# A two-layer diffusion step: 80 conditioning sums spread over four places instead of three, and one SiLU moved behind the first query copy

## The chip, the cores and the metric

The kernel runs on one core of a Trainium2 chip. The metric is the device time of one execution in microseconds (us); lower is better. The kernel has hand-written instruction streams for the engines: TensorE (PE in the profile), VectorE (DVE), ScalarE (ACT), GpSimd (POOL) and SyncE (SP). They meet only at semaphores. SP, ACT and POOL also issue DMAs.

## The reference, cut to what matters

A sequence of 128 prompt tokens and 256 latent tokens goes through two layers. Layer 0 has an mLSTM mixer, layer 1 a Mamba-2 (SSD) mixer, and each is followed by a mixture of experts. Every sub-layer is modulated by vectors that come from a conditioning vector:

```python
for i in range(DEPTH):
    mp = (jax.nn.silu(c_ctx) @ ada_w[i] + ada_b[i]).reshape(6, D_MODEL)   # prompt stream
    ms = (jax.nn.silu(c) @ ada_w[i] + ada_b[i]).reshape(-1, 6, 1, D_MODEL)  # latent stream
    hp = xp * (1.0 + mp[1]) + mp[0]
    ...   # mixer: mLSTM (i = 0) or SSD (i = 1)
    xp = _layer_norm(ALPHA * xp + mp[2] * yp, ln_w[i, 0], ln_b[i, 0])
    fp = _hier_moe(xp * (1.0 + mp[4]) + mp[3], *wm)
    xp = _layer_norm(ALPHA * xp + mp[5] * fp, ln_w[i, 1], ln_b[i, 1])

def _mlstm_mixer(h, ...):
    xu, z = jnp.split(h @ w_in, 2, axis=-1)
    xc = jax.nn.silu(_dwconv(xu, conv_w, conv_b))
    q, k, v = blockdiag(xc, w_q), blockdiag(xc, w_k), blockdiag(xu, w_v)
    gates = jnp.concatenate([q, k, v], axis=-1) @ w_gates + b_gates
    ...
```

The first mixer's shift and scale need two of layer 0's six vectors; those are made by TensorE at the start. The other ten vectors of 1024 numbers (four of layer 0, six of layer 1), for both streams, are the subject of the change.

## The kernel before, in words

**The conditioning sums.** The ten vectors are cut into 80 slabs of 128 outputs. A slab is a 128x1024 piece of the transposed weight (512 KB), and VectorE makes its 128 outputs for a stream as one multiply of the slab with the SiLU of the conditioning row, summed along the row by the same instruction (L1925). So a slab costs two such instructions, one per stream, each waited for. `summed(place, n)` does the next n slabs; `biased(l, j0, j1)` adds the bias to finished entries. POOL issues the loads: `columns(place)` (L1368) first loads the two conditioning rows (`c_rows`, 1 MB since they are spread to 128 partitions), then each slab into one of four slots of the place, and slab i may be issued only when sum i-3 is done. ScalarE makes the SiLU of the rows once for each place (`c_silu`, L1545).

There are three places, with `COLUMNS = (14, 42, 24)` slabs, each with its own rows and slots in parts of the arena that are free at that time:

- place 0: during the first mixer's up-projection and convolution, one slab behind each of the convolutions 1 to 14;
- place 1: four slabs ahead of, sixteen inside (one for each channel tile) and twenty-two behind the loop that multiplies the mLSTM's output with its gate, so during the z projection and the down-projection of the first mixer;
- place 2: during the down-projection of the second mixer.

In place 1 the slab whose index is a multiple of four goes to a slot that also holds the row of normaliser states; POOL waits for that row's DMA to the output (`out_mn`) before it issues such a slab.

**The first mixer's front.** TensorE projects 16 channel tiles of `xu` two at a time (L581). For each, ScalarE copies the tile out of PSUM and makes the middle tap (L1538 to L1543), VectorE adds four taps (L1949), ScalarE applies SiLU (L1534, L1535). When the projection is done, TensorE makes q, k and v of tile 0 and 1 and then, for each tile, gate products (L866), a transpose of v (L872) and q, k, v of the tile after next (L882, L886). The gate products of tile c wait for the copies of q and v by ScalarE (L1564, L1568) and of k by VectorE (L1961). ScalarE's stream is in order: the SiLU of tile 15 stands ahead of the first copy of q. POOL builds the block-diagonal weights (L1387).

**The first mixer's end.** TensorE projects z (L581), with two transposes of the mLSTM output behind each pair; VectorE combines them (L2113, L2117) and does a sum. Then the down-projection (L601) goes over two halves of 512 outputs and three token tiles; `gate_rows` (L625) stands three steps into it and needs VectorE's `diagonals` (L2138). VectorE's sums of the last 22 slabs stand ahead of `mixed(0)`, which takes the down-projection's banks, adds the residual and normalises (L2169 to L2153); TensorE then transposes the result (L633). PSUM banks are claimed in a ring of five or six; a claim waits for the last reader of what the bank held.

**The second mixer's front.** The residual comes from the experts; L1646 (ScalarE) and L2187 (VectorE) write the modulated input. TensorE projects 24 tiles of B, C and x in twelve steps (L581); behind the first stands the step-size projection (L1040), behind the fourth the transposes `columns()` (L1052 to L1058), which need VectorE's chain of softplus, scans and `rows_done` (L2445 to L2476). VectorE does a convolution per tile (L1949), ScalarE the copies and SiLU. ScalarE's wait for the softplus input (L1743) stands right behind `a_neg` (L1741). Meanwhile POOL multiplies and shifts the residual stream by the norm's weights (`new_x(1)`, L1398 and L1399, six instructions) and clears the convolution's pads.

SP issues the weight slabs into a ring of six (L1300) and the experts' weights (L1239, L1266). It waits for the sums of the first two places before it loads experts' slab 5 of layer 0.

## Time and profile before

| | |
|---|---|
| median of 3 runs | 1394.72 us (1389.98 to 1398.69) |
| profiled execution, its own time | 1389.08 us |
| its span, first to last instruction | 1387.2 us |
| mean granted TensorE clock | 0.932 of full |
| PE busy | 1214.7 us (88%) |
| DVE busy | 707.3 us (51%) |
| ACT busy | 369.0 us (27%) |
| POOL busy | 207.2 us (15%) |
| DMA | 290.17 MB, mean 209 GB/s |

All row times are microseconds from the span's start. A timeline row is: start, length, engine, line, operation, output<-input, count, and in brackets the idle time of the engine ahead of it with what ended it. A chain row is: start, length, what the end of the execution was waiting for at that time. The busy share is an average over stages; what counts below is which wait ends last in each stage.

### The profile page before, as it was taken

To read this page: it belongs to the slowest core of one execution; us is meant where nothing else is said; L and a number is where in the kernel's file an instruction comes from. 1 tells how busy PE (TensorE), PEld (TensorE's weight loads), DVE (VectorE), ACT (ScalarE), POOL (GpSimd) and SP (SyncE) were. 2 spreads that over 40 slices of the span, in tenths; PEclk is the share of its full clock that TensorE was granted. 3 is DMA by queue.
4 is the path that set the end of the run, shared out by engine and by line. 5 is a ranking of instruction groups with operands and counts; after the bars stand their busy time and mean duration, and the time that the engine had idled before them with its cause. 6 is when DMAs were issued, how large, how long until landed. Compare 5 with 4: busy or idle time off the path is not lost.

```text
span 1387.2 us, 14709 instructions
## 1 busy us (share of the span) xinstructions
PE 1214.7 (88%) x5174; PEld 659.8 (48%) x5174; DVE 707.3 (51%) x1538; ACT 369.0 (27%) x808; POOL 207.2 (15%) x307
## 2 busy tenths in 40 slices
PE   5898978999999797899585999989998999899573
PEld 2554545554566343734222555656666444743221
DVE  0399244342476599541104365448885777541014
ACT  1433331222300000311013354444555211311011
POOL 5012200000010010002201401003334110002201
PEclk9999997999999899799798999999999899799796
DMA  9553001327397486299936332234435697399934
GB/s 375 191 192 135 1 1 49 114 108 260 128 388 256 153 345 245 89 415 422 420 155 219 137 122 84 93 107 152 141 126 170 214 381 297 129 416 421 421 146 149
DMA packets 75844, 290.17 MB, mean 209 GB/s; under 512 B 7692, under 2 KB 18188, under 8 KB 61436
## 3 DMA queue, kind: packets, MB, share of 16 engines
q1 hardware_dynamic: 41952, 191.12, 35.7%
q0 software_dynamic: 16352, 60.44, 11.8%
q10 hardware_dynamic: 17468, 37.67, 7.4%
q8 instruction: 42, 0.69, 0.2%
q14 instruction: 30, 0.25, 0.1%
HBM read 261.30 MB, written 27.90 MB: 208 GB/s over the span
## 4 chain that ended last, share of the span: by engine, by line
PE 63%; DVE 12%; DMA 11%; issue 9%; ACT 4%; SPq 1%; POOL 0%; ACTq 0%; POOLq 0%; DVEq 0%
PE bank L581 19%; PE bank L740 7%; PE bank L601 7%; DMA arena<-in_moe_gu 4%; PE bank L949 4%; DVE arena L1925 3%; PE bank L760 3%; PE bank L1136 3%; DMA ring<-in_ada_w 3%; DVE arena L2501 2%; DVE arena L1949 2%; PE bank L840 2%; PE bank L882 1%; DMA ring<-in_b_w_out 1%; PE bank L977 1%
## 5 line engine op out<-in xcount | busy, mean ns | idle before, releaser
L581 PE MATMUL bank<-hT,ring 128*128 128x384 f32 x896 | 297.9, 494 | 3.8 <-ACT hT L1525 1.7
L581 PEld LDWEIGHTS bank<-hT,ring 128*128 128x128 f32 x896 | 172.0, 194 | 122.0 <-issue 6.8
L601 PE MATMUL bank<-ring,arena 128*128 128x512 f32 (+1 forms) x512 | 178.2, 614 | 9.1 <-DVE arena L2113 7.3
L1925 DVE SCALAR_TENSOR_TENSOR arena<-arena 128x1024 f32<-128x1024 f32 x112 | 137.3, 1226 | 6.9 <-DMA arena<-in_ada_wT 4.2
L740 PE MATMUL bank<-arena,hT 128*64 128x512 f32 x416 | 107.4, 637 | 34.0 <-DMA arena<-in_moe_gu 22.7
L1949 DVE SCALAR_TENSOR_TENSOR arena<-arena,par 128x388 f32<-128x388 f32 x160 | 101.6, 638 | 67.4 <-ACT arena L1543 62.8
L601 PEld LDWEIGHTS bank<-ring,arena 128*128 128x128 f32 (+1 forms) x512 | 73.9, 198 | 103.7 <-issue 87.0
L1136 PE MATMUL bank<-hT,ring 128*128 128x384 f32 x256 | 97.6, 507 | 0.8 <-ACT arena L1543 0.8
L740 PEld LDWEIGHTS bank<-arena,hT 128*64 128x64 f32 x416 | 37.7, 146 | 92.1 <-issue 86.5
L1380 POOL DMA_DIRECT2D arena<-in_ada_wT x74 | 39.1, 529 | 272.3 <-DVE arena L1925 266.1
L1470 POOL TENSOR_TENSOR arena<-arena 128x192 f32<-128x192 f32 x64 | 42.7, 697 | 214.0 <-PE bank L1169 156.7
L2317 DVE TENSOR_TENSOR arena<-arena,bank 128x256 f32<-128x256 f32 x16 | 6.7, 422 | 127.3 <-ACT arena L1669 127.3
L2569 DVE TENSOR_TENSOR arena<-arena 128x1024 f32<-128x1024 f32 x32 | 42.0, 1311 | 35.6 <-ACT arena L1814 35.6
L949 PE MATMUL bank<-ring,arena 128*128 128x512 f32 x128 | 58.3, 616 | 0.0
L1136 PEld LDWEIGHTS bank<-hT,ring 128*128 128x128 f32 x256 | 44.8, 192 | 26.4 <-issue 8.7
L2501 DVE TENSOR_SCALAR arena<-arena 128x128 f32<-128x128 f32 x192 | 49.9, 328 | 4.0 <-PE bank L1169 4.0
L760 PE MATMUL bank<-arena 128*64 128x512 f32 x208 | 50.7, 592 | 0.0
L1925 DVE SCALAR_TENSOR_TENSOR arena<-arena,hT 128x1024 f32<-128x1024 f32 x36 | 44.1, 1224 | 3.4 <-DMA arena<-in_ada_wT 2.3
L1669 ACT ACTIVATE arena<-bank 128x256 f32<-128x256 f32 x16 | 6.1, 383 | 145.0 <-PE bank L740 145.0
L1810 ACT ACTIVATE arena<-arena 128x768 f32<-128x768 f32 x32 | 27.0, 844 | 66.1 <-DVE arena L2501 66.1
L840 PE MATMUL bank<-arena,hT 128*128 128x512 f32 x48 | 25.3, 692 | 19.6 <-DMA arena<-yg,slots 19.6
L949 PEld LDWEIGHTS bank<-ring,arena 128*128 128x128 f32 x128 | 25.0, 198 | 30.2 <-issue 30.1
(425 smaller groups left out, 1656.5 us busy)
## 6 DMA issues: line engine op xcount, KB each, us to landing
arena<-in_moe_gu SPq DMA_DIRECT2D x56, 1024.0 KB, 15.8
arena<-in_ada_wT POOLq DMA_DIRECT2D x74, 512.0 KB, 5.6
arena<-in_moe_dn SPq DMA_DIRECT2D x28, 1024.0 KB, 20.8
ring<-in_b_w_in SPq DMA_DIRECT2D x40, 512.0 KB, 3.5
ring<-in_a_w_in SPq DMA_DIRECT2D x32, 512.0 KB, 6.4
ring<-in_moe_gu SPq DMA_DIRECT2D x12, 1024.0 KB, 14.4
arena<-acs_rows ACTq DMA_DIRECT2D x32, 384.0 KB, 3.5
yg<-arena ACTq DMA_DIRECT2D x18, 512.0 KB, 8.1
```

What stands on the lines that cost most here:

```text
L581: last = mm(keys[j][1][:, 0:T], w[:, k, P * j:P * j + P], hT[:, 4 * half + k, :], start=half == 0 and k == 0, stop=half == 1 and k == 3, s ...
L601: last = mm(keys[t][1][p:p + tokens.shape[1], :], tokens, w[:, j, :], start=k == 0, stop=k == KE - 1, skip_group_check=True)
L740: last = mm(ps[CAP * u:CAP * u + CAP, :], m_hg[:, q % 2, P * k + CAP * u:P * k + CAP * u + CAP], v3(w[u][1], 4)[:, j, :], start=k == 0, st ...
L760: last = mm(ps[CAP * u:CAP * u + CAP, :], m_aT[:, P * f + CAP * u:P * f + CAP * u + CAP], v3(w[u][1], 2)[:, f, 512 * h:512 * h + 512], sta ...
L840: last = mm(ps[:, :], w_diag[:, t, i, :], m_y[:, i, t, 512 * half:512 * half + 512], start=i == 0, stop=i == 1)
L949: last = mm(keys[t - 1][1][:, :], a_qT[:, KH * h + 2 * half + j, P * t:P * t + P], w[:, j, :], start=half == 0 and j == 0, stop=half == 1 ...
L1136: last = mm(ps[:, 0:T], v3(w, 4)[:, k % 4, P * (c % 2):P * (c % 2) + P], hT[:, k, :], start=k == 0, stop=k == KD - 1, skip_group_check=True)
L1470: ins = pl.tensor_tensor(out=b_xdt[c % 2][:, d, :, PH * h:PH * h + PH], in0=b_x[:, :, P * c + PH * h:P * c + PH * h + PH], in1=b_col[:, o: ...
L1925: ins = ve.scalar_tensor_tensor(out=products, in0=c_slots[place][i % 4], scalar=1.0, in1=rows[:, v, :], op0=ALU.mult, op1=ALU.mult, accum_ ...
L1949: last = ve.scalar_tensor_tensor(out=dst, in0=src[:, j:j + W_PAD - 2 * PAD], scalar=w(j), in1=dst, op0=ALU.mult, op1=ALU.add)
L2501: ins = ve.tensor_scalar(b_E[:, h, d, P * t:P * t + P], b_row[:, m % 3, h, P * t:P * t + P], b_col[:, at:at + 1], 0.0, ALU.add, ALU.min)
L2569: ve.tensor_tensor(out=e, in0=e, in1=b_cb[:, g % 2, d, :].unsqueeze(1).to_broadcast([P, 2, 512]), op=ALU.mult).then_inc(sem("w_ready"), 1)
```

## The change

The 80 sums are done in four places, `COLUMNS = (12, 36, 8, 24)`. The order of the slabs stays.

- Place 0 has 12 slabs: convolutions 13 and 14 have none behind them.
- Place 1 has 36: four ahead of the gate loop, twelve inside it (every fourth tile has none), twenty behind it. Its first slab now has index 12, a multiple of four.
- A new place 2 has 8 slabs, in the second mixer's front: four right behind `modulated(1)` and ahead of the softplus chain, and one behind each of the convolutions 6 to 9. Their bias is added behind convolution 10. ScalarE's SiLU of the rows stands between `a_neg` and the softplus. POOL loads the rows and the first four slabs when the experts' results are gathered, ahead of `new_x(1)`; it loads the other four behind `new_x(1)` and the pads, and waits for all eight sums before it goes on to `xdt`.
- The former place 2 is place 3, with its 24 slabs as before.
- ScalarE's SiLU of tile 15 stands behind the first copies of q and v instead of ahead of them.

```diff
--- before.py
+++ after.py
@@ -200,13 +200,16 @@
         free = lambda o, n=D: arena[:, o:o + n]
         q_at = KE * T + KE * W_PAD
         gone_at, far_at = KE * T + 4 * D, ARENA - 7 * D
-        c_rows = [v3(a, 2) for a in (free(q_at, 2 * D), free(far_at + 5 * D, 2 * D), hT_free[:, 0:2 * D])]
-        c_products = (free(q_at + 2 * D), free(far_at + 4 * D), free(KE * T + 2 * D))
+        later = KE * T + 2 * G * T + NT * E2
+        e_at = later + NT * E2 + 2 * E2 + ZT * T + 3 * 2 * T + 2 * NT * P + T + 9 * 64
+        c_rows = [v3(a, 2) for a in (free(q_at, 2 * D), free(far_at + 5 * D, 2 * D), free(e_at, 2 * D), hT_free[:, 0:2 * D])]
+        c_products = (free(q_at + 2 * D), free(far_at + 4 * D), free(e_at + 3 * D), free(KE * T + 2 * D))
         c_slots = [[free(o + D * i) for i in range(4)] for o in (q_at + 3 * D, far_at)]
+        c_slots.append([free(o) for o in (later - D, later + 2 * P * KD, e_at - T - 9 * 64 - 2 * NT * P - 2 * T, e_at + 2 * D)])
         c_slots.append([free(gone_at), free(gone_at + D), hT_free[:, 2 * D:3 * D], free(ARENA - 12 * MSLAB)])
-        COLUMNS = (14, 42, 24)
+        COLUMNS = (12, 36, 8, 24)
         column_of = [(place, l, j) for place, (l, j) in zip(
-            [p for p in range(3) for _ in range(COLUMNS[p])], [divmod(2 * KD + i, 48) for i in range(80)])]
+            [p for p in range(4) for _ in range(COLUMNS[p])], [divmod(2 * KD + i, 48) for i in range(80)])]
         COLUMN_SEMS = ("pool_in0", "pool_in1", "pool_in2", "xc_in0")
 
         def column_landed(i):
@@ -216,7 +219,7 @@
 
         def columns_in(l, j):
 
-            return 16 * len(range(j, sum(COLUMNS[0:2 + l]), 4))
+            return 16 * len(range(j, sum(COLUMNS[0:2 + 2 * l]), 4))
 
         def rows_landed(l, t):
 
@@ -1365,13 +1368,14 @@
 
             pool.wait_ge(sem("small_in"), SMALL)
 
-            def columns(place):
+            def columns(place, n0=0, n1=None):
 
                 first = sum(COLUMNS[0:place])
-                pool.wait_ge(sem("small_in"), SMALL + 16 * place)
-                pool.dma_start(c_rows[place].rearrange("p v k -> p (v k)"),
-                               i_["c_rows"].to_broadcast([P, 2 * D])).then_inc(sem("small_in"), 16)
-                for i in range(first, first + COLUMNS[place]):
+                if n0 == 0:
+                    pool.wait_ge(sem("small_in"), SMALL + 16 * place)
+                    pool.dma_start(c_rows[place].rearrange("p v k -> p (v k)"),
+                                   i_["c_rows"].to_broadcast([P, 2 * D])).then_inc(sem("small_in"), 16)
+                for i in range(first + n0, first + (n1 or COLUMNS[place])):
                     _, l, j = column_of[i]
                     if i >= 4:
                         pool.wait_ge(sem("summed"), i - 3)
@@ -1456,9 +1460,14 @@
                 pool.wait_ge(sem(f"out{s}"), 16 * OUT_C)
             columns(1)
             moe(0)
+            for t in range(NT):
+                pool.wait_ge(*rows_landed(0, t))
+            columns(2, 0, 4)
             new_x(1, range(NT))
             pl.memset(b_cbuf.rearrange("p k t -> p (k t)"), 0.0)
             pl.memset(b_pre.rearrange("p k t -> p (k t)"), 0.0).then_inc(sem("pads"), 1)
+            columns(2, 4)
+            pool.wait_ge(sem("summed"), sum(COLUMNS[0:3]))
 
             def xdt(c):
                 pool.wait_ge(read("xt"), c + 1)
@@ -1489,7 +1498,7 @@
             pool.wait_ge(sem("xdt_ready"), 2 * KE)
             pool.wait_ge(sem("wx_ready"), 2 * G)
             pool.wait_ge(filled, group["in", 3 * KE - 1][1])
-            columns(2)
+            columns(3)
             moe(1)
 
 
@@ -1557,7 +1566,6 @@
                     conv_silu(c - 1, a_cbuf[:, (c - 1) % 2, :], a_cb(c - 1), a_xc[:, c - 1, :], "xc_ready")
                 if c == 0:
                     c_silu(0)
-            conv_silu(KE - 1, a_cbuf[:, (KE - 1) % 2, :], a_cb(KE - 1), a_xc[:, KE - 1, :], "xc_ready")
 
             for c in range(KE):
                 ps = await_bank(act, "qT", c)
@@ -1566,6 +1574,8 @@
                 if c >= 2:
                     act.wait_ge(filled, group["v", c - 2][1])
                 ac(a_vb[:, c % 2, :], ps[:, 0:T], ACT.Copy).then_inc(read("vT"), 1)
+                if c == 0:
+                    conv_silu(KE - 1, a_cbuf[:, (KE - 1) % 2, :], a_cb(KE - 1), a_xc[:, KE - 1, :], "xc_ready")
 
 
             act.wait_ge(sem("softplus_x"), 1)
@@ -1739,6 +1749,7 @@
             modulated(1, 2)
 
             ac(a_neg[:, :], a_log[:, :], ACT.Exp).then_inc(sem("dt_a"), 1)
+            c_silu(2)
             act.wait_ge(sem("softplus_x"), 2)
             link(ac(b_u, b_u, ACT.Exp))
             ac(b_l, b_u, ACT.Ln, bias=1.0).then_inc(sem("softplus_ln"), 1)
@@ -1859,9 +1870,9 @@
                 if m >= 26:
                     new_state(m - 26)
             z_silu(12, 15)
-            c_silu(2)
             new_state(6)
             new_state(7)
+            c_silu(3)
             for c in range(10, KE):
                 normed(c)
             scaled(KE - 1)
@@ -1953,9 +1964,9 @@
             for c in range(KE):
                 dve.wait_ge(read("in"), c + 1)
                 conv(c, a_xu[:, c, :], a_cbuf[:, c % 2, :], lambda j: a_cw(j, c), "conv_ready")
-                if 0 < c < KE - 1:
+                if 0 < c < 13:
                     summed(0, 1)
-            biased(0, 16, 30)
+            biased(0, 16, 28)
             for c in range(KE):
                 ps = await_bank(dve, "kT", c)
                 ve.tensor_copy(a_kT[:, c, :], ps[:, 0:T]).then_inc(read("kT"), 1)
@@ -2115,7 +2126,8 @@
                 dve.wait_ge(read("hn"), c + 1)
                 dve.wait_ge(read("in"), KE + c + 1)
                 ve.tensor_tensor(out=xc, in0=xc, in1=a_sz[:, c, :], op=ALU.mult).then_inc(sem("gA_ready"), 1)
-                summed(1, 1)
+                if c % 4 != 3:
+                    summed(1, 1)
 
             def columns(n):
 
@@ -2433,12 +2445,13 @@
             dve.wait_ge(sem("out_mn"), 32)
             dve.wait_ge(sem("x_in"), 16 * (MAXOQ + 1))
             diagonals(0)
-            summed(1, 22)
-            biased(0, 30, 48)
-            biased(1, 0, 24)
+            summed(1, 20)
+            biased(0, 28, 48)
+            biased(1, 0, 16)
             mixed(0, "yA")
             moe(0)
             modulated(1)
+            summed(2, 4)
 
 
             ps = await_bank(dve, "single", 3)
@@ -2548,6 +2561,10 @@
                 w = 16 + c if c < 8 else c - 8
                 dve.wait_ge(read("xbc"), c + 1)
                 conv(c, b_pre[:, c % 4, :], b_cbuf[:, c % 3, :], lambda j: b_cw(j, w), "conv_ready")
+                if 6 <= c < 10:
+                    summed(2, 1)
+                if c == 10:
+                    biased(1, 16, 24)
                 if c == 4:
                     rows_done()
                 elif c == 5:
@@ -2587,12 +2604,12 @@
             dve.wait_ge(sem("c_in"), 16 * (1 + OUT_S))
             dve.wait_ge(sem("par_in"), 16 * (2 + OUT_S))
             diagonals(2, (0, 1))
-            summed(2, 12)
+            summed(3, 12)
             diagonals(2, (2, 3))
-            summed(2, 2)
+            summed(3, 2)
             ps = await_bank(dve, "single", 4)
             ve.tensor_scalar(rms, ps[:, 0:NT], float(D) / E2, EPS, ALU.mult, ALU.add).then_inc(read("single"), 1)
-            summed(2, 10)
+            summed(3, 10)
             biased(1, 24, 48)
             dve.wait_ge(sem("sqrt_ready"), 2)
             link(ve.reciprocal(rms, rms))
```

## Rows read from the trace of the kernel before

**Rows 1.** The page: shares of the span in the chain that ended last.

```profile
PE 63%; DVE 12%; DMA 11%; issue 9%; ACT 4%; SPq 1%; POOL 0%; ACTq 0%; POOLq 0%; DVEq 0%
```

**Rows 2.** Chain of waits, end of the first mixer's convolutions.

```profile
137.79 0.40 ACT arena L1534
...
138.59 0.37 ACT arena L1564
138.96 0.39 ACT arena L1568
```

**Rows 3.** Timeline there, VectorE and ScalarE.

```profile
124.67 2.60 DVE L1949 SCALAR_TENSOR_TENSOR arena<-arena,par 128x388 f32<-128x388 f32 x4
127.19 1.22 DVE L1925 SCALAR_TENSOR_TENSOR arena<-arena 128x1024 f32<-128x1024 f32 x1
...
127.45 0.49 ACT L1543 ACTIVATE arena<-bank,par 128x256 f32<-128x256 f32 x1
...
130.03 0.49 ACT L1543 ACTIVATE arena<-bank,par 128x256 f32<-128x256 f32 x1
```

**Rows 4.** Timeline of TensorE, the gate products that follow.

```profile
139.59 1.50 PE L866 MATMUL bank<-arena,gates_w 128*32 128x384 f32 x6 [6.15 <-ACT arena L1568]
...
145.05 0.85 PE L866 MATMUL bank<-arena,gates_w 128*32 128x384 f32 x6
...
148.26 0.85 PE L866 MATMUL bank<-arena,gates_w 128*32 128x384 f32 x6
```

**Rows 5.** Windows there: PE, PEld, DVE, ACT, POOL busy (x), clock, DMA, GB/s.

```profile
139.60:141.70 2.10, 2.10 (x9) 0.86 (x10) 0.00 (x0) 0.50 (x2) 0.00 (x0) 0.50 0.00 0
```

**Rows 6.** Timeline, start of place 1: POOL, VectorE, TensorE.

```profile
372.80 1.06 POOL L1380 DMA_DIRECT2D arena<-in_ada_wT  x2
380.06 1.05 POOL L1380 DMA_DIRECT2D arena<-in_ada_wT  x2 [6.20 <-DMA out_n<-arena]
...
387.41 1.23 DVE L1925 SCALAR_TENSOR_TENSOR arena<-arena 128x1024 f32<-128x1024 f32 x1 [2.99 <-DMA arena<-in_ada_wT]
...
400.32 10.49 PE L581 MATMUL bank<-hT,ring 128*128 128x384 f32 x32
```

**Rows 7.** Timeline, the first down-projection: VectorE and TensorE.

```profile
482.51 0.69 DVE L2138 TENSOR_TENSOR arena<-ident,mod 128x512 f32<-128x512 f32 x1 [11.43 <-PE bank L625]
...
485.07 60.25 PE L601 MATMUL bank<-ring,arena 128*128 128x512 f32 x140
552.35 1.97 PE L633 MATMUL bank<-ident,x_tok 128*128 128x128 f32 x8 [7.03 <-DVE x_tok L2153]
554.11 5.20 PE L601 MATMUL bank<-ring,arena 128*128 128x512 f32 x8
```

**Rows 8.** Timeline, second mixer's front: VectorE's gap, ScalarE, POOL.

```profile
783.02 0.61 DVE L2445 TENSOR_SCALAR arena<-bank,dt_bias 64x384 f32<-64x384 f32 x1 [16.80 <-PE bank L1040]
...
767.53 0.20 ACT L1741 ACTIVATE a_neg<-a_log 64x1 f32<-64x1 f32 x1
...
776.75 2.35 POOL L1399 TENSOR_TENSOR x_tok<-x_tok,arena 128x1024 f32<-128x1024 f32 x1
```

**Rows 9.** Timeline and chain: VectorE and POOL on the arena together.

```profile
113.26 2.18 POOL L1387 TENSOR_TENSOR arena<-arena 128x128 f32<-128x128 f32 x6
...
113.11 2.76 DVE arena L1949
...
131.57 5.10 POOL L1387 TENSOR_TENSOR arena<-arena 128x128 f32<-128x128 f32 x6 [16.13 <-PE bank L886]
...
132.32 1.41 DVE L1925 SCALAR_TENSOR_TENSOR arena<-arena 128x1024 f32<-128x1024 f32 x1
```

**Rows 10.** Timeline, what TensorE's fifth projection step needs.

```profile
810.34 0.28 DVE L2476 TENSOR_TENSOR arena<-arena 64x128 f32<-64x128 f32 x1
...
812.28 0.49 ACT L1543 ACTIVATE arena<-bank,par 128x256 f32<-128x256 f32 x1
...
814.77 20.91 PE L581 MATMUL bank<-hT,ring 128*128 128x384 f32 x64
```

## The prediction

> **What bounds the kernel now.** I read the chain of waits first. Two thirds of the span hang on TensorE and only 12% on VectorE [rows 1], so the 80 slab sums matter only in the stages where VectorE is the last to arrive. There the timelines of all engines show who waits. Two such places are emptied by the change, and a third is filled.
>
> One slab costs 2.53 us of VectorE: a sum starts at 127.19, and the convolution behind it can start at 129.71 [rows 3].
>
> **Front of the first mixer (a gain).** The chain runs through VectorE's last convolution, then ScalarE's SiLU of tile 15 from 137.79 and its first copies of q and v, to 139.35 [rows 2]; TensorE then starts its gate products at 139.59, after 6.15 us of idling [rows 4]. Without the sums behind convolutions 13 and 14 the taps are held back by their input instead. ScalarE frees tile 14 at 127.45 + 0.4 = 127.9 and tile 15 at 130.03 + 0.4 = 130.4 [rows 3]. Convolution 15 then takes 2.5 us (124.67 to 127.19, [rows 3]) and ends at 133.0, against 137.8 before. Behind the new order ScalarE copies q and v of tile 0 while VectorE still works on tile 15, at about 131.3 to 132.2, so the last to arrive is VectorE's copy of k: bias 0.2, copy 0.55 (lengths from the timeline), 133.8. The gate products start at 133.85 instead of 139.59: 5.7 us. Of these 4.7 are the two sums and about 1 is the moved SiLU, which stood as 0.8 us ahead of 0.75 us of copies [rows 2].
>
> There is a second part. Behind the 6.15 us of idling TensorE ran at a granted clock of 0.50, the level of 1.2 GHz [rows 5], and its first round took 145.05 - 139.59 = 5.46 us against 3.21 for the next, at full clock [rows 4]. TensorE would be busy until 133.4 and idle for 0.4 us only, so I expect no fall: 2.2 us more (0 if it falls anyhow). Together **-7.9 us** (bounds -5.7 and -7.9; the loop behind it is a TensorE loop of 3.2 us per tile and passes the gain on).
>
> **Start of place 1 (a loss).** Before, POOL issued slabs 14 and 15 at 372.80 and had to wait for the state row's DMA only for slab 16, at 380.06 [rows 6]. Now the first slab is number 12, a multiple of four, so nothing but the rows is issued before 380.06, and 13, 14, 15 stand in POOL's queue behind that wait. Slab 16 landed at 387.4, 7.3 us after its issue: VectorE waited 2.99 us for it [rows 6]. Slab 12 will land then, and VectorE, which before had two sums behind it by 387.4, has all four ahead of it: it enters the gate loop at 397.7 instead of 392.5. In the loop VectorE has 3.7 us of idling in each pair and tile 3 now has no sum (2.5 us), so it catches up by tile 4. But the projection step at 400.4 [rows 6] needs the bank that VectorE frees in tile 1, at 397.7 + 3.7 + 0.6 = 402.0 (0.6 is the combining instruction). TensorE waits for it: **+1.6 us**. Below, 0: if the lone slab lands 2 us sooner. Above, 4: if the following slabs, with DMA engines full, land late once more each. The nearest row is the 7.3 us, hence 1.6.
>
> At the loop's end nothing is won: tiles 12, 13, 14 have the same sums as before, and TensorE waits for tile 14's bank. The sum saved behind tile 15 only lengthens VectorE's idle 11.43 us ahead of the diagonals [rows 7].
>
> **Behind the first down-projection (a gain).** From 484 to 541 VectorE does 22 sums in one row, while TensorE's projection ends at 485.07 + 60.25 = 545.3 [rows 7]. `mixed(0)` follows, 10.8 us to the first normalised tile, and TensorE idles 7.03 us until 552.35 [rows 7]. Twenty sums end 2 x 2.53 = 5.1 us sooner. The first token tile's second half is projected by 538.4, before VectorE comes to it (543.7), so the whole 5.1 us arrive, and 2.0 us of idling stay. SP's wait for the first two places' sums comes 5.1 us sooner too. The clock again: the eight records behind the idling took 5.20 us [rows 7] where eight at the projection's pace of 60.25 / 140 = 0.43 take 3.4. VectorE's next tile is ready only 5.1 us sooner, so of this at most 1.4 can be used; I take half: **-5.8 us** (-5.1 to -6.5).
>
> **Second mixer's front (the price).** VectorE has 16.80 us of nothing there, until TensorE has the step sizes at 783.02 [rows 8]. Four sums are 10.1 us. Their slabs and rows, 3 MB, are issued from 750.3 on, when the gathered results have landed and DMA engines are empty; they are there by 762. ScalarE's SiLU costs a table load (1.28) and 1.91 us (as in place 1) behind 767.53 + 0.20 [rows 8]: VectorE starts at 771.0, and without anything else it would end at 781.1. These 10.1 us would be free.
>
> But POOL works through `new_x(1)` until 779.1 [rows 8], 2.35 us per instruction, on SBUF operands like VectorE's. When six of POOL's small instructions ran back to back for 2.18 us, a tap of 0.63 took 2.76: VectorE lost all of POOL's time [rows 9]. When VectorE was in sums, POOL was the one that waited (5.10 for the same six), and a sum lost 0.19 [rows 9]. Here POOL has 8.0 us left at 771, and VectorE's eight instructions outlast it. Bounds for VectorE's loss are 4 x 0.19 = 0.8 and 8.0 us. I take 7.5: POOL's instructions are long, two stand back to back, and each lets one of VectorE's through at most.
>
> The Trainium skill, SBUF - State Buffer, section "SBUF: two separate sides", says that a VectorE instruction with two SBUF inputs and a GpSimd one that reads SBUF exclude each other for a whole instruction, whoever was first, and that the loser is blocked fully. By it the loss would be the full 8.0 us; the sum that lost only 0.19 beside a POOL instruction of 0.36 shows less than that.
>
> VectorE ends at 788.6 and the softplus chain is 5.5 us late. It is a chain through ScalarE and back, and up to convolution 5 it has almost no idling, so all of it moves. TensorE has slack: `rows_done` was ready at 810.6 for a use at 814.1 (3.5 us), and tile 6, whose bank the fifth step needs, was copied at 812.28 + 0.49 = 812.8, for a start at 814.8 (2.0 us) [rows 10]. So TensorE waits 5.5 - 2.0 = 3.5 us: **+3.4 us** (bounds 0 and 4.5).
>
> The other four sums, behind convolutions 6 to 9, add 10.1 us. VectorE idles 3.24, 5.14 and 5.56 us ahead of convolutions 8, 10 and 12 (timeline), 13.9 in all. Worked through tile by tile, with 5.5 us of lateness TensorE's 3.5 us of waiting make room, and convolution 12 starts when its input comes. Their cover is this idling; without it they would cost what VectorE overruns. Their slabs are issued at about 784 and needed from 818. POOL's wait for all eight sums ends at about 840, and its first `xdt` needs a transpose of that time anyway. Bias 0.2 us: hidden. The other place-3 work is as before. Zero.
>
> **The sum** against the profiled execution's own 1389.08: -7.9 + 1.6 - 5.8 + 3.4 = -8.7, so 1380.4. That execution stood 5.6 us below the median shown; against the median of 1394.72 it is **1386 us**, -0.6%. What a measurement of this kernel can tell from no change is about 1%, 14 us; the three runs alone spread over 8.7.
>
> **Rivals.**
> - *POOL and VectorE don't hold each other up* (the sum that lost 0.19 speaks for it, the tap that lost 2.13 against). The second mixer's front costs nothing, and with the start of place 1 at 0 to 1.6 the whole is -12.1 to -13.7: 1381 to 1382.6. Chance 0.25.
> - *Given back*: the sums in place 1 start late and stay late (slabs 16 to 19 took 7.3 to 10.6 us to land), TensorE waits in two or three of its steps instead of one (+4), the clock falls as before (the 2.2 and the 0.7 are lost), and the front costs its 4.5. Then -5.7 + 4 - 5.1 + 4.5 = -2.3: 1392. Chance 0.16.
> - *Slower*: the second mixer's front becomes bound by VectorE. Place: convolutions 6 to 12. Price: all eight sums, 20.3, and POOL's 8.0 on TensorE's path, less the 13.4 won elsewhere: about +15, 1410. It decides if VectorE reaches convolution 12 later than its input, which from the sums above needs over 5 us more than I count. For it: VectorE and ScalarE pass each other every tile there. Against it: 13.9 us of idling in the same stretch. Chance 0.07.
> - My forecast (1382 to 1390) has the remaining 0.52.
>
> **Numbers.** The range takes the rivals of gain, the bounds, and 4 us of scatter of the median: 1376 to 1397; only the slow rival lies outside. Faster by over 1% (below 1380.8): half of the first rival, and a tenth of the forecast for scatter and unused clock gains, and the tails: 0.23. Slower by over 1%: 0.07. Within: 0.70.
>
> **What would show it.** (1) The idling ahead of the first gate products shrinks from 6.15 to under 1 us, and the first round takes 3.2 us. (2) The first sum of place 1 starts at the new time that answers to 387.4, and one z step waits for VectorE. (3) Idling ahead of the first L633 is about 2 us. (4) In the second mixer's front VectorE's sums beside `new_x(1)` have instructions of 3 us and more, and the softplus input comes about 5.5 us behind TensorE's step sizes; TensorE waits once ahead of its fifth step. The prediction is wrong if those sums run at 1.22 us each, if a stage behind them (the experts) takes back what was won, or if TensorE waits for VectorE in convolutions 8 to 12.

## The result and the profile after

The changed kernel takes 1374.55 us (median of 4 runs, 1373.22 to 1377.01) against 1394.43 for the kernel before in the same comparison: ratio 0.986, interval 0.983 to 0.989. Three later comparisons, on three chips, gave 0.987 (0.985 to 0.990), 0.989 (0.986 to 0.992) and 0.989 (0.987 to 0.992). On the four chips of the experiments the kernel before has a median of 1391.5 us (74 runs; 1391.7 with the four of the first comparison), and the kernel after, over all its 21 runs, one of 1375.0. So the change is worth 16.6 us, 1.2%. I had predicted 1386, 8.7 us less than before, and the result lies 1.5 us below my range.

The page of the profiled execution (span 1375.2, own time 1377.01), first the chain that ended last; line numbers are 3 to 13 higher than before.

```profile
PE 60%; DMA 12%; DVE 12%; issue 9%; ACT 5%; SPq 1%; POOL 0%; ACTq 0%; POOLq 0%; DVEq 0%
```

Nothing has moved by much against [rows 1]: TensorE is still the bound. The change shows in single waits. **The first gate products**, timeline of TensorE, start, length, line and, in brackets, the idle time before:

```profile
134.40 0.85 PE L869 MATMUL bank<-arena,gates_w 128*32 128x384 f32 x6 [0.74 <-issue]
...
137.60 0.85 PE L869 MATMUL bank<-arena,gates_w 128*32 128x384 f32 x6
```

They answer to [rows 4]: 0.74 us of idling in place of 6.15, and the first round takes 3.20 us where it took 5.46. Its six matmuls last 0.85 us instead of 1.50, the length that they have at the full clock. **The start of place 1**, POOL, VectorE and TensorE:

```profile
372.18 2.28 POOL L1384 DMA_DIRECT2D arena<-in_ada_wT  x4 [6.04 <-DMA out_n<-arena]
...
380.08 1.22 DVE L1936 SCALAR_TENSOR_TENSOR arena<-arena 128x1024 f32<-128x1024 f32 x1 [7.29 <-DMA arena<-in_ada_wT]
...
395.83 1.56 PE L584 MATMUL bank<-hT,ring 128*128 128x384 f32 x4 [1.48 <-DVE arena L2124]
```

Against [rows 6] POOL issues all four slabs in one go behind its wait, VectorE waits 7.29 us for the first, and one z step waits 1.48 us for a bank. **The first down-projection**, TensorE, answering to [rows 7]:

```profile
543.61 1.31 PE L636 MATMUL bank<-ident,x_tok 128*128 128x128 f32 x8 [3.58 <-DVE x_tok L2165]
544.72 5.13 PE L604 MATMUL bank<-ring,arena 128*128 128x512 f32 x8
```

The same place in the trace of after_again, a second profiled execution of the changed kernel (experiment 1):

```profile
540.77 1.12 PE L636 MATMUL bank<-ident,x_tok 128*128 128x128 f32 x8 [1.74 <-DVE x_tok L2165]
541.73 3.60 PE L604 MATMUL bank<-ring,arena 128*128 128x512 f32 x8
```

3.58 or 1.74 us of idling are left of 7.03. The eight matmuls behind it took 5.20 us before; they take 3.60 where the granted clock is full (1.00 over that stretch of after_again), and 5.13 where it isn't (0.72 in the first trace). **The second mixer's front**, VectorE's eight sum instructions with POOL's `new_x(1)` beside them, the step sizes (L2458), and TensorE's wait ahead of its fifth step, answering to [rows 8, 10]:

```profile
761.43 2.04 DVE L1936 SCALAR_TENSOR_TENSOR arena<-arena 128x1024 f32<-128x1024 f32 x1 [4.79 <-ACT arena L1557]
763.51 3.24 DVE L1936 SCALAR_TENSOR_TENSOR arena<-arena 128x1024 f32<-128x1024 f32 x1
766.80 3.24 DVE L1936 SCALAR_TENSOR_TENSOR arena<-arena 128x1024 f32<-128x1024 f32 x1
770.09 3.25 DVE L1936 SCALAR_TENSOR_TENSOR arena<-arena 128x1024 f32<-128x1024 f32 x1
773.38 1.23 DVE L1936 SCALAR_TENSOR_TENSOR arena<-arena 128x1024 f32<-128x1024 f32 x1
...
778.45 0.61 DVE L2458 TENSOR_SCALAR arena<-bank,dt_bias 64x384 f32<-64x384 f32 x1
```

```profile
760.03 2.36 POOL L1402 TENSOR_TENSOR x_tok<-x_tok,arena 128x1024 f32<-128x1024 f32 x1
762.47 3.21 POOL L1403 TENSOR_TENSOR x_tok<-x_tok,arena 128x1024 f32<-128x1024 f32 x1
765.63 3.33 POOL L1402 TENSOR_TENSOR x_tok<-x_tok,arena 128x1024 f32<-128x1024 f32 x1
769.04 3.21 POOL L1403 TENSOR_TENSOR x_tok<-x_tok,arena 128x1024 f32<-128x1024 f32 x1
...
806.12 0.28 PE L1055 MATMUL bank<-ident,arena 64*128 64x64 f32 x1 [1.03 <-DVE arena L2489]
...
807.86 1.53 PE L584 MATMUL bank<-hT,ring 128*128 128x384 f32 x4 [0.97 <-ACT arena L1552]
```

Four of the eight instructions ran beside POOL and took 11.8 us instead of 4.9. TensorE then waits twice, 1.03 us for `rows_done` and 0.97 for its bank.

**Landmarks.** Each row is a stretch between two instructions of TensorE, in the us of one profiled execution of each kernel. "Before" has two executions and "after" four, so the last columns give the scatter too; "others" are experiments (below) that don't touch the stretch, or that have it as the kernel before has it where that is said.

| stretch, by the times of before | before | after | others |
|---|---|---|---|
| start to 194.3 (front) | 194.3, 195.6 | 186.8, 186.3, 186.2, 187.3 | old front 193.7, 194.9 |
| 194.3 to 366.4 (scan) | 172.1, 174.1 | 173.4, 172.9, 172.5, 174.1 | 172.0 to 173.9 |
| 366.4 to 400.3 (place 1 starts) | 33.9, 35.4 | 35.6, 35.7, 35.3, 35.6 | old order 33.8, 33.8 |
| 400.3 to 552.4 (to the router) | 152.0, 150.7 | 147.8, 145.9, 147.0, 146.0 | 22 sums 151.8 |
| 552.4 to 765.3 (experts 0) | 213.0, 214.9 | 212.1, 212.9, 213.5, 213.4 | 210.9 to 213.5 |
| 765.3 to 814.8 (step sizes) | 49.5, 49.9 | 52.1, 51.7, 52.1, 52.1 | no sums 49.4, 49.4 |
| 814.8 to 909.9 (convolutions) | 95.1, 95.1 | 95.1, 96.8, 95.1, 95.1 | 95.1, 96.8 |
| 909.9 to 1121.6 (end of mixer 2) | 211.7, 209.1 | 207.5, 207.7, 207.7, 207.9 | below |
| 1121.6 to the end (experts 1) | 265.6, 265.5 | 264.8, 263.3, 260.8, 266.4 | 263.5 to 268.5 |

The two profiled executions that were there first differ by 12.1 us only (1389.08 and 1377.01). The one of before lies 2.4 us below the median of its kernel, the one of after 2.0 above: this is the rest of the 16.6.

### The profile page after: what moved, and what is told of

It reads as the page before. It is cut to its first block, busy times and chain, and to the rows that moved or that the text cites. A ratio compares the mean times of both kernels' runs of the same rounds, so it can differ in the third digit from the quotient of the medians.

```text
span 1375.2 us, 14716 instructions
## 1 busy us (share of the span) xinstructions
PE 1206.2 (88%) x5174; PEld 654.0 (48%) x5174; DVE 712.4 (52%) x1539; ACT 373.3 (27%) x811; POOL 212.4 (15%) x308
## 3 DMA queue, kind: packets, MB, share of 16 engines
q0 software_dynamic: 16496, 61.49, 11.8%
## 4 chain that ended last, share of the span: by engine, by line
PE 60%; DMA 12%; DVE 12%; issue 9%; ACT 5%; SPq 1%; POOL 0%; ACTq 0%; POOLq 0%; DVEq 0%
PE bank L584 16%; PE bank L604 9%; PE bank L743 7%; DMA arena<-in_moe_gu 4%; PE bank L952 4%; PE bank L763 3%; PE bank L1139 3%; DMA ring<-in_ada_w 3%; DVE arena L1936 2%; DVE arena L2514 2%; PE bank L843 2%; PE bank L885 2%; DMA out_C<-arena 1%; PE bank L980 1%; DMA ring<-in_b_w_out 1%
## 5 line engine op out<-in xcount | busy, mean ns | idle before, releaser
L604 PE MATMUL bank<-ring,arena 128*128 128x512 f32 (+1 forms) x512 | 175.3, 608 | 8.9 <-DVE arena L2124 7.2
L1936 DVE SCALAR_TENSOR_TENSOR arena<-arena 128x1024 f32<-128x1024 f32 x112 | 144.1, 1287 | 19.0 <-DMA arena<-in_ada_wT 11.4
L1479 POOL TENSOR_TENSOR arena<-arena 128x192 f32<-128x192 f32 x64 | 42.8, 699 | 208.9 <-PE bank L1172 154.0
L2586 DVE TENSOR_TENSOR arena<-arena 128x1024 f32<-128x1024 f32 x32 | 41.7, 1304 | 35.3 <-ACT arena L1825 35.3
```

What stands on the lines that cost most here:

```text
L604: last = mm(keys[t][1][p:p + tokens.shape[1], :], tokens, w[:, j, :], start=k == 0, stop=k == KE - 1, skip_group_check=True)
L1479: ins = pl.tensor_tensor(out=b_xdt[c % 2][:, d, :, PH * h:PH * h + PH], in0=b_x[:, :, P * c + PH * h:P * c + PH * h + PH], in1=b_col[:, o: ...
L1936: ins = ve.scalar_tensor_tensor(out=products, in0=c_slots[place][i % 4], scalar=1.0, in1=rows[:, v, :], op0=ALU.mult, op1=ALU.mult, accum_ ...
L2586: ve.tensor_tensor(out=e, in0=e, in1=b_cb[:, g % 2, d, :].unsqueeze(1).to_broadcast([P, 2, 512]), op=ALU.mult).then_inc(sem("w_ready"), 1)
```

## The experiments

Sixteen runs, in four groups that each shared a chip and the runs of the kernel before. A ratio is to that kernel.

**1. Both kernels again.** No edit.

> The kernel before once more, unchanged, to learn how far its own executions differ. The profiled difference of the two kernels was 12.1 us, the difference of the medians 19.9. If the 7.8 us between them are scatter of the kernel before, its five rounds here lie between about 1389 and 1399 again, and its landmarks in the trace move in the stages that wait for DMA alone. If they are a real gain of the change that the two profiled executions happened not to show, the profiled execution here is at about 1395 and the landmarks of the first mixer are later than in the first trace.

> The kernel after once more, unchanged. Theory of the scatter: 1373 to 1379, a ratio of 0.987 to 0.991 (12 to 18 us). Rival, a real gain of 20: ratio 0.985 to 0.986.

Measured: 1391.59 (1.000, 0.998 to 1.002) and 1374.58 (0.987, 0.985 to 0.990), 17 us apart; their profiled executions, 1392.03 and 1374.96, are 17.1 apart. The landmarks of before are up to 3.3 us later at the end of the scan, and 1.5 more at the start of place 1. The gain is about 17 us, inside the 12 to 18 of the scatter theory; the interval doesn't rule out the rival's 0.986. So the 12.1 of the first pair of traces was chance, and so were the 19.9 of the first medians. Repeats of after, as partners on the chips of groups 3 and 4:

> The kernel after, unchanged, on the same chip as the three others: 1373 to 1378, ratio 0.986 to 0.989.

> The kernel after, unchanged, on the same chip as the others: 1372 to 1378.

Measured: 1375.39 (0.989, 0.986 to 0.992) and 1376.23 (0.989, 0.987 to 0.992).

**2. The last SiLU of the second mixer.** The diff moves it from ahead of `new_state(6)` and `new_state(7)` to behind them. Edit of silu_move_only, in the kernel before; silu_move_undone (and its repeat silu_undone_again) does the reverse in the kernel after.

```diff
             z_silu(12, 15)
-            c_silu(2)
             new_state(6)
             new_state(7)
+            c_silu(2)
```

> The kernel before with one edit: at the end of the second mixer its last SiLU over the gates stands behind the last two states on ScalarE instead of ahead of them. My theory of the miss: in the trace before, this SiLU waits 2.59 us for its data from DMA, the scaling of the last states queues behind it, and PE waits 3.07 for that; with the SiLU moved, the down-projection's first part starts about 6.7 earlier, 2.5 of it is given back at the gate's rows, whose diagonals then wait for DMA, and about 4.2 us stay: ratio 0.997, 2 to 6 us faster than before. Rival (the 4 us come from the sums that no longer run there, not from the SiLU): 0, within 1.5 us of before, and the first part of the down-projection starts where it did.

> The kernel after with this one edit undone: the last SiLU over the gates stands ahead of the last two states again. My theory: 4.2 us slower than after (2 to 6), ratio to before 0.991 to 0.994, and the scaling of the last states waits on ScalarE behind the SiLU. Rival (the SiLU's move is worth nothing without the sums' lateness): within 1.5 us of after.

> The kernel after with the second mixer's last SiLU ahead of its last two states again, repeated: the first time its median was 7.1 us above that of the kernel after on the same chip, while the two traces showed 3 to 5. If the SiLU's place is worth what the traces show (the states' products wait 3.8 us for ScalarE; some of it given back at the gate's rows), 3 to 5 us slower than after_third; rival, 7 again, because the idling also makes the clock fall in some executions that the profiled one does not show: then the mean granted clock of its timed runs is lower, by 0.003 or more, than that of after_third.

Measured: silu_move_only 1387.59 (0.997, 0.995 to 0.999) on the chip where before had 1391.89, so 4.3 us faster. silu_move_undone 1381.70 (0.993, 0.990 to 0.995) where after had 1374.58; the repeat 1379.87 (0.990, 0.989 to 0.992) where after had 1375.39, so 7.1 and 4.5 slower. Over the twelve runs its median is 1380.3, 5.4 above after's. In the trace of before_again, timeline of ScalarE and then of TensorE:

```profile
1079.13 1.91 ACT L1548 ACTIVATE hT<-hT 128x2048 f32<-128x2048 f32 x1 [2.49 <-DMA hT<-in_c_rows]
1080.94 0.58 ACT L1799 ACTIVATE arena<-bank 128x512 f32<-128x512 f32 x1
```

```profile
1081.67 1.36 PE L1119 MATMUL bank<-arena 128*128 128x128 f32 x8 [3.79 <-ACT arena L1799]
1082.82 1.91 PE L601 MATMUL bank<-ring,arena 128*128 128x512 f32 x2
```

The SiLU waits 2.49 us for its rows from DMA and runs 1.91. The state's copy (L1799) stands behind it in ScalarE's queue, TensorE waits 3.79 us for that copy, and the down-projection (L601) stands behind both. Nothing needs the SiLU at that point: VectorE reads it for sums that come later. The same stretch of silu_move_only:

```profile
1074.61 0.58 ACT L1799 ACTIVATE arena<-bank 128x512 f32<-128x512 f32 x1
...
1079.72 1.91 ACT L1548 ACTIVATE hT<-hT 128x2048 f32<-128x2048 f32 x1 [0.46 <-ACT arena L1799]
```

```profile
1076.71 1.92 PE L1119 MATMUL bank<-arena 128*128 128x128 f32 x8
1078.47 1.88 PE L601 MATMUL bank<-ring,arena 128*128 128x512 f32 x4
```

Here the wait is gone. The wait had a second cost: behind it the down-projection's first twenty matmuls ran at a lower granted clock. They are shown for the kernel before (0.75), then for the kernel after (1.00):

```profile
1079.44 7.26 PE L601 MATMUL bank<-ring,arena 128*128 128x512 f32 x20
```

```profile
1065.79 5.53 PE L604 MATMUL bank<-ring,arena 128*128 128x512 f32 x20
```

All five traces with the SiLU ahead show 7.01 to 7.27 us for them, twelve of the thirteen with it behind 5.53 and one 5.71. But not all of this arrives. Counted from 909.9 the down-projection begins at 162.9 us in the kernel after, at 166.8 and 167.0 with only the SiLU put back (silu_move_undone and its repeat), at 167.2 and 169.6 in the kernel before and at 166.4 in silu_move_only. So at that point the SiLU's place is worth some 4 us in the kernel after, and 2.8 are given back behind the down-projection's first part:

```profile
1107.20 3.43 PE L628 MATMUL bank<-arena,ones 128*128 128x512 f32 x4 [2.82 <-DVE arena L2150]
```

```profile
1074.84 1.29 DVE L2150 TENSOR_TENSOR arena<-ident,mod 128x512 f32<-128x512 f32 x2 [7.44 <-DMA out_s<-arena]
```

VectorE's diagonals (L2150) wait 7.44 us for the store of the last states, the gates' rows (L628) wait 2.82 for the diagonals, and this is the new bound of the place. From 909.9 to 1121.6 the five traces with the SiLU ahead show 208.8 to 211.7 us (mean 210.0), thirteen with it behind 207.5 to 209.6 (mean 207.9): 2.1 us. That mean mixes two kernels. In the kernel after alone the stretch takes 208.8 and 208.9 us with the SiLU ahead and 207.5 to 207.9 behind, 1.2 us. Counted from 909.9 to the end of the span the means of the five and the thirteen are 476.7 and 473.1, 3.6 us, but single traces overlap there (474.5 to 480.1 and 468.4 to 476.6). The timed effect is larger, 4.3 to 7.1. My second rival for that, a lower clock in runs that no trace shows, expected 0.003 between the means; the repeat had 0.941 against 0.942, the first run 0.940 against 0.942. So it is shown that the SiLU's place costs time and by which wait; the size is 1 to 4 us by the traces and 4 to 7 by the times, and where the difference lies stays open.

**3. The front of the first mixer.** front_undone is the kernel after with the old front, front_only the kernel before with the new one.

```diff
 front_undone, against after:
-        COLUMNS = (12, 36, 8, 24)
+        COLUMNS = (14, 34, 8, 24)
-                if 0 < c < 13:
+                if 0 < c < KE - 1:
-            summed(1, 20)
+            summed(1, 18)
...
 front_only, against before:
-        COLUMNS = (14, 42, 24)
+        COLUMNS = (12, 44, 24)
-                if 0 < c < KE - 1:
+                if 0 < c < 13:
-            summed(1, 22)
+            summed(1, 24)
```

In both the bounds of `biased` follow the sums, and the SiLU of tile 15 stands as in the front that they take over.

> The kernel after with the front of the first mixer as before: 14 sums behind its convolutions, the SiLU of tile 15 ahead of the first copies of q and v, and 18 sums instead of 20 behind the first down-projection (place 1 gets 34 slabs, its first is number 14). My theory of the front: TensorE idles 6 us again ahead of its first gate product, its clock falls for the first round, and the gates end 7.5 to 8 us later than in the kernel after. Behind the down-projection two sums fewer should take away the 1.7 to 3.6 us of idling that the kernel after still has there (the last to arrive is then TensorE), and place 1 starts as before, with two slabs issued ahead of the wait for the state row: -1.5. So 3 to 6 us slower than after: ratio to before 0.990 to 0.992. Rival (the front's gain is given back later, and the whole gain of the change lies in the second mixer and the down-projection): within 1.5 us of after, or faster.

> The kernel before with the front of the first mixer alone changed as in the kernel after: 12 sums behind its convolutions, the SiLU of tile 15 behind the first copies of q and v; the two slabs go to place 1 (44), as two more sums behind the first down-projection (24). My theory: the front gives 8 us (gates end at about 186.5 instead of 194.2 to 195.6), the start of place 1 takes 1.5 back, and VectorE's 24 sums in one row end two sums later than in the kernel before, so that 5 us go there: the idling ahead of the router's first transposes grows from 6.6 to about 12. In all 1 to 2 us faster than before: ratio 0.999. Rival, the down-projection's length is set by DMA and not by the sums: 6 to 7 us faster, 0.995.

Measured: front_undone 1380.03 (0.993, 0.991 to 0.995), front_only 1389.81 (0.9995, 0.998 to 1.001). The first lies just above the 0.990 to 0.992 of my theory, which its interval holds; it shuts out the rival. The second is near the theory's 0.999, and shuts out the rival's 0.995. TensorE's first gate products in the trace of front_undone:

```profile
139.11 1.50 PE L869 MATMUL bank<-arena,gates_w 128*32 128x384 f32 x6 [6.16 <-ACT arena L1577]
140.54 0.90 PE L875 MATMUL bank<-ident,arena 128*128 128x128 f32 x3
141.24 2.67 PE L885 MATMUL bank<-arena 128*128 128x384 f32 x4
```

Idling and the slow round are back together, and the first landmark comes at 193.7 against 186.2 to 187.3. In front_only it comes at 185.7, some 9 us earlier than in the kernel before. But ahead of the router's first transposes, TensorE in front_only:

```profile
554.01 1.97 PE L633 MATMUL bank<-ident,x_tok 128*128 128x128 f32 x8 [13.82 <-DVE x_tok L2154]
```

13.82 us of idling against 7.03 [rows 7]: that stretch takes 159.2 us instead of 151.5. The front's gain is a real one, and two slabs that are only pushed into the next place cost nearly all of it there: 7.7 us, and 1.4 at the start of place 1, of the 9. That eight slabs go on to a place of their own lets it arrive.

**4. The moved SiLU of tile 15.** Edit of qv_undone, in the kernel after:

```diff
+            conv_silu(KE - 1, ..., "xc_ready")
             for c in range(KE):
                 ps = await_bank(act, "qT", c)
...
-                if c == 0:
-                    conv_silu(KE - 1, ..., "xc_ready")
```

> The kernel after with one edit: the SiLU of tile 15 stands ahead of the first copies of q and v again. By the sum of the prediction this is worth about 1 us (VectorE's copy of k for the first tile is then not the last; 0.8 us of SiLU stands ahead of 0.75 us of copies): the first gate product 0.8 to 1 us later, and no fall of the clock. Rival: with 1.7 us of idling in place of 0.74 the clock falls for the first round as it did before, and 3 us are lost.

Measured: 1377.57 (0.990, 0.988 to 0.993). TensorE:

```profile
134.39 0.85 PE L869 MATMUL bank<-arena,gates_w 128*32 128x384 f32 x6 [1.58 <-ACT arena L1577]
```

1.58 us of idling against 0.74: 0.84 us, and the matmuls keep their 0.85. The rival is out.

**5. The start of place 1.** Edit of rotated, in the kernel after:

```diff
-        c_slots = [[free(o + D * i) for i in range(4)] for o in (q_at + 3 * D, far_at)]
+        c_slots = [[free(q_at + 3 * D + D * i) for i in range(4)], [free(far_at + D * ((i + 1) % 4)) for i in range(4)]]
-                    if place == 1 and i % 4 == 0:
+                    if place == 1 and i % 4 == 3:
```

> The kernel after with the slots of place 1 rotated by one, so that the slab that must wait for the state row's DMA is the fourth issued and no longer the first. Theory: the first sum of place 1 starts as VectorE comes free (7 us of waiting for its slab go), VectorE enters the gate loop earlier, and the z step that waits 1.5 us for its bank in the kernel after waits for nothing: -1.5 us, ratio 0.986. Rival: the later slabs land late instead, with the DMA engines as full as before, and nothing changes (within 0.5 us at the end of the z steps).

Measured: 1376.21 (0.991, 0.988 to 0.994), which tells nothing of 1.5 us. The trace does: POOL issues three slabs before the wait,

```profile
363.58 1.76 POOL L1384 DMA_DIRECT2D arena<-in_ada_wT  x3
372.25 0.53 POOL L1384 DMA_DIRECT2D arena<-in_ada_wT  x1 [6.91 <-DMA out_n<-arena]
```

VectorE starts its sums at 370.15 without waiting, no z step waits for a bank, and the stretch takes 34.0 us against 35.3 to 35.7 (with waits of 1.10 to 1.75) in the kernel after. A second trace with the rotation gave 33.9, a third 35.2 (both and packed, below), again with no wait. The third has its 1.3 us elsewhere: the first 64 matmuls of the stretch took 23.68 us instead of 22.40 and 22.57.

**6. POOL beside the sums.** Edit of no_new_x, in the kernel after:

```diff
-                    x = x_tok[:, t, :]
-                    link(pl.tensor_tensor(out=x, in0=x, in1=rows[:, 0, :], op=ALU.mult))
-                    pl.tensor_tensor(out=x, in0=x, in1=rows[:, 1, :], op=ALU.add)...
+                    x = x_tok[:, t, 0:8 if n == 1 else D]
+                    link(pl.tensor_tensor(out=x, in0=x, in1=rows[:, 0, 0:8 if n == 1 else D], op=ALU.mult))
+                    pl.tensor_tensor(out=x, in0=x, in1=rows[:, 1, 0:8 if n == 1 else D], op=ALU.add)...
```

> The kernel after, but POOL's new_x(1) works on 8 of 1024 columns: it leaves out nearly all of the scaling and shifting of the second mixer's residual rows. This takes POOL's work away from beside VectorE's sums and leaves everything else. Theory of the mutual hold-up: the sums' instructions are 1.23 us again instead of 3.24, VectorE ends 6.9 us earlier, the step sizes are no longer late, and TensorE's fifth step comes 2.7 us earlier: ratio 0.985. Rival (the instructions are longer for another reason, such as the slabs' landing in SBUF): they stay above 2 us and nothing moves.

Measured: 1376.03 (0.990, 0.988 to 0.992). VectorE's sums in its trace:

```profile
759.10 1.23 DVE L1936 SCALAR_TENSOR_TENSOR arena<-arena 128x1024 f32<-128x1024 f32 x1 [5.08 <-ACT arena L1557]
...
767.97 1.23 DVE L1936 SCALAR_TENSOR_TENSOR arena<-arena 128x1024 f32<-128x1024 f32 x1
...
771.67 0.61 DVE L2458 TENSOR_SCALAR arena<-bank,dt_bias 64x384 f32<-64x384 f32 x1 [2.47 <-PE bank L1043]
```

All eight take 1.22 or 1.23 us, VectorE waits for TensorE again, and the stretch to the fifth step takes 49.9 us instead of 51.7 to 52.1. So POOL's work is the cause, and costs 2.2 us on the path. The time doesn't show it: the stretches behind scatter by more. The price has a second part that comes and goes. In three of the ten traces with TensorE's two waits (after_again, front_undone, silu_move_undone) the 64 matmuls behind them take 22.57 us instead of 20.88, and the convolutions' stretch 96.8 instead of 95.1; in after_again the granted clock was 0.79 over the first 8 us, in the first trace of after 1.00. In the eight traces without these waits it is 95.1 each time.

**7. Three sums ahead of the softplus.** Edit of three_ahead, in the kernel after; both adds the rotation of experiment 5.

```diff
             modulated(1)
-            summed(2, 4)
+            summed(2, 3)
...
-                if 6 <= c < 10:
+                if 6 <= c < 11:
```

> The kernel after with three of the second mixer's eight sums ahead of the softplus instead of four, the fifth behind convolution 10. By the hold-up between POOL's scaling and VectorE's sums, VectorE comes 2.5 us sooner to the step sizes (lateness 5.0 to about 2.5), TensorE's fifth step starts about 2 us earlier, and the five sums behind convolutions 6 to 10 stay hidden: 1.5 to 2.5 us faster than after. Rival: the eighth sum behind convolution 10 is not hidden, VectorE holds TensorE up in the convolutions, and the time is as after or up to 2.5 us more.

> Three sums ahead of the softplus and the slots of place 1 rotated, together. The rotation alone took 1.6 us off the first z steps in its trace (366 to 400), three sums ahead should take off 2: 3.5 us faster than after, ratio 0.984, the fastest of all. Rival: what is won ahead of the experts is given back there, where TensorE waits 10 us for weights from DMA: then the fifth step of the second mixer is 3.5 us earlier and the end less than 1.5.

Measured: three_ahead 1374.43 (0.986, 0.984 to 0.989), both 1374.30 (0.986, 0.984 to 0.989), against 1375.39 for after on that chip. The stretch to the fifth step is 49.6 us in both, as without any sums there, and the convolutions keep their 95.1. Up to the fifth step the 2.3 us are there; at the end about 1 is seen, within the scatter. The rival (given back in the experts) can't be told from it.

**8. What is left behind the first down-projection.** Edit of packed_alone, in the kernel after; packed is both with the same edit.

```diff
-                if c % 4 != 3:
-                    summed(1, 1)
+                summed(1, 1)
...
-            summed(1, 20)
+            summed(1, 16)
```

> Rotated slots, three sums ahead of the softplus, and in place 1 a sum behind each of the 16 tiles of the gate loop instead of 12, with 16 behind the first down-projection instead of 20. VectorE idles 6.0 and 3.8 us by turns in that loop, so the four sums fit (10 us into some 25 of idling), and without them the down-projection's end is set by TensorE: the 1.7 to 3.6 us of idling ahead of the router's transposes go, with a fall of the clock behind it. 2 to 3 us faster than the version without it (both), 5 faster than after in the trace up to the experts. Rival: the gate loop is held up by VectorE, and the z steps grow by up to 2.5 us a pair. What reaches the end is what the experts' wait for weights leaves.

> The kernel after with the 16 and 16 sums of place 1 alone (no rotation, four sums ahead of the softplus). 2 to 3 us faster than after up to the experts, if the four moved sums hide in the gate loop although VectorE enters it 1.5 us late; if they don't, a second z step waits for its bank and 1 to 2.5 us of it are lost.

Measured: packed 1375.00 (0.989, 0.986 to 0.992), packed_alone 1371.33 (0.988, 0.985 to 0.990), after 1376.23 on that chip. TensorE in packed_alone, around the place where the idling was:

```profile
534.49 6.17 PE L604 MATMUL bank<-ring,arena 128*128 128x512 f32 x14
540.49 1.04 PE L636 MATMUL bank<-ident,x_tok 128*128 128x128 f32 x8
```

No idling is left. The stretch to the router is 143.8 us in both kernels (after: 145.9 to 147.8), and the experts behind it take 208.7 and 208.9 us instead of 212.1 to 213.5: some 7 us in two stretches, more than the 2 to 3 expected. Of the 4 us in the experts one possible cause is on view: SP issues the experts' slabs that wait for place 1's sums at 519.76 in packed and 522.81 in packed_alone, against 532.14 in the kernel after. No run takes that apart. The medians show 5 and 1 of them, with the intervals overlapping. The four sums hide in the gate loop, where VectorE idles 6 and 4 us by turns. packed_alone has the lowest median and packed the fastest single execution (1365.36); a version that surely beats the changed kernel is not shown by times, only by the traces up to the second mixer.

## Why the prediction was wrong

The step that failed is one sentence, in the part on the second mixer's front: "The other place-3 work is as before. Zero." The diff moves a SiLU past two `new_state` there, in ScalarE's queue, and I priced it at nothing without looking at what stood behind it. The trace of before had the answer: 2.6 us of waiting for the rows, 1.9 of SiLU, and TensorE waiting 3.07 us at 1077.60 for the copy behind it:

```profile
1075.06 1.91 ACT L1548 ACTIVATE hT<-hT 128x2048 f32<-128x2048 f32 x1 [2.59 <-DMA hT<-in_c_rows]
...
1077.60 2.05 PE L1119 MATMUL bank<-arena 128*128 128x128 f32 x8 [3.07 <-ACT arena L1799]
```

Experiment 2 puts 5.4 us of time on it, two thirds of the 7.9 that are missing between my 8.7 and the 16.6 measured; the traces show less of it, 2.1 us in its own stretch and 3.6 counted to the end.

The other steps, from the means of the traces that share a stretch:

| step | predicted | traces | what differed |
|---|---|---|---|
| front of the first mixer | -7.9 | -8.1 (194.6 to 186.5) | right, clock and all |
| start of place 1 | +1.6 | +1.2 (34.2 to 35.5) | right; one trace of before holds 1.5 us of slow matmuls |
| first down-projection, up to its transposes | -5.1 | -4.6 (151.5 to 146.9) | the sums waited longer for slabs |
| the clock behind it | -0.7 | -1.8 (11.0 to 9.2) | mostly full again, not half |
| second mixer's front | +3.4 | +2.3 (49.6 to 51.9) | VectorE lost 6.9, not 7.5; TensorE's slack was 2.6, not 2.0 |
| convolutions | 0 | +0.5 (95.1 to 95.6) | slow matmuls in three traces of ten |
| last SiLU of place 3 | 0 | -2.1 (210.0 to 207.9) | overlooked; -4.3 to -7.1 by times |

- **Front.** The mechanism was right in both halves: experiment 3 takes the 6.16 us of idling and the 2.2 of the slow round away and back together.
- **Start of place 1.** The mechanism was right: a z step waits 1.10 to 1.75 us for its bank in all four traces of after, and the late lone slab causes it (experiment 5). The stretch is as long in the second trace of before for another reason. There no step waits, though slab 16 landed 3.72 us late instead of 2.99, but TensorE's first 64 matmuls took longer. Before, then before_again:

```profile
366.38 22.47 PE L581 MATMUL bank<-hT,ring 128*128 128x384 f32 x64 [0.90 <-ACT arena L1610]
```

```profile
369.66 23.95 PE L581 MATMUL bank<-hT,ring 128*128 128x384 f32 x64 [1.49 <-ACT arena L1610]
```

The granted clock was 0.60 and then 1.00 in the first and second 4 us of the one, 0.50 and 0.73 in those of the other.

- **Down-projection.** The term was 0.6 too small in all, by two errors that cancel in part. The stretch up to the first transposes shrank by 4.6, not 5.1. I had each sum following the last at 2.53 us; in the first trace of after, VectorE also waits 2.0 and 0.8 us for slabs in that row of sums (1.2 in the trace before). And I took half of the clock's 1.4. From the first transposes to the router's first matmul TensorE takes 10.8 to 11.2 us in three traces with 22 sums, and with 20 sums 9.0 in nine traces of eleven and 10.4 in two, so 1.8 on average. With 24, 22, 20, 18 and 16 sums the stretch takes 159.2, 151.5, 146.9, 144.7 and 143.8 us: each pair is worth less than the one before, down to where TensorE is the last to arrive.
- **Second mixer's front.** The price was real, and the rival that denied it (no hold-up) is out by experiment 6. The pairs of instructions follow each other every 3.29 us; alone they take 1.23 and 2.35, together 3.58. So VectorE and POOL took turns almost fully, with 0.3 us of overlap in a pair, and both lost. The Trainium skill, SBUF - State Buffer, section "SBUF: two separate sides", has the loser blocked for the whole instruction of the other. By it VectorE's loss would have been, as an estimate from the POOL work that was left when the sums began, 8.0 us; the trace shows 6.9, close but smaller. TensorE waited twice, not once: `rows_done`, to which I gave 3.5 us of slack, came 1.03 us late too.
- **The rivals.** None of the three happened: POOL did hold VectorE up, nothing was given back in the gate loop, and convolutions 6 to 12 hide their sums (TensorE's waits in them are the same 0.83 and 0.63 us with and without them). The time came out beyond my rival of gain (1381 to 1382.6), whose mechanism is out. All four of my cases left the same thing out. The slow rival's price has a slip in its sum: the other terms win 12.1, not 13.4, so that it is +16 and not +15.
- **The base.** I compared with a median of three runs, 1394.72; over 74 runs it is 1391.5. The absolute time predicted would have been 3 us lower, and still 8 too high. With it my range would have moved down by 3 as well and held the time; the gain would still have been half of the measured one.

The steps add up to -10.5 us without the SiLU, to -12.6 with its 2.1, to -14.1 with the 3.6 that the traces show to the end, and to -15.9 with its 5.4 of the times. So 0.7 to 4 us of the 16.6 stay unplaced; the experts' stretches, which differ by up to 6 us between executions of one kernel, are wide enough to hold them, but no run shows it.

## What to carry to other kernels

Go through a diff by queues, not by the topic of its title: every instruction that changes its place in an in-order queue is a change of its own, and what counts is what stood behind it and what it was waiting for. Optional work that waits for a DMA belongs behind the instruction that the critical engine needs. A gain that only moves work into the next stage's full engine is none (experiment 3), so follow the moved work to where it has real idling around it.

## What the runs showed of the hardware

- A VectorE sum of 1024 elements with both operands in SBUF and a POOL operation of 1024 elements, also in SBUF, alternate: 1.23 and 2.35 us alone, 3.24 and 3.21 to 3.33 beside each other. POOL lost time too, 0.9 us an instruction: neither side simply wins.
- With idling of 0.74 or 1.58 us ahead of the first gate products (fourteen traces) the granted clock stayed at the 2.4 GHz level (0.85 us for six matmuls); with 6.15 and 6.16 us it was at the 1.2 GHz level (1.50 us), in four traces of four.
- At other places the length of the idling alone doesn't tell. Ahead of the router's transposes 3.09 and 3.58 us were followed by a low clock (eight matmuls in 5.30 and 5.13 us), 3.38 us, and eight idlings of 1.74 to 2.69, by the full one (3.60). Ahead of the second mixer's fifth step three traces fell with waits of 0.58 to 0.82 and 0.97 us (64 matmuls in 22.57 us), and seven with 1.02 or 1.03 and 0.97 didn't (20.88).
- One profiled execution of the kernel before or after lies up to 5.6 us from the median of its comparison (1389.08 and 1394.72). The mean granted clock of a run goes with its time: over the first 23 runs of before it lies between 0.928 (1397.59 and 1393.99 us) and 0.941 (1385.82 us).
